# A hybrid mixer in a fused two-block kernel: attention heads taken in pairs, mask and pattern counts added in PSUM by TensorE, and the attention half of the output product multiplied first

## The chip, the cores and the metric

The kernel runs on one core of one Trainium2 chip. The metric is the device time of one execution in microseconds (us); smaller is better. Before the change the median of three runs was 2360.88 us, the lowest 2359.72 and the highest 2361.94.

## What is computed

One program holds two networks' blocks on 256 tokens of width 1024: a first block (retention, a gated spatial unit, and two expert layers that gather rows from memory) and then a second block. The change is in the hybrid mixer of the second block only:

```
def hybrid_mixer(h, w_in, conv_w, g_attn_out, g_conv_out, w_out):
    proj = h @ w_in                                   # 1024 -> 6 x 512
    q, k, v, bg, cg, xc = jnp.split(proj, 6, axis=-1) # 8 heads of 64
    for window, dilation in ((128, 1), (512, 4), (2048, 16)):
        o, lse = dilated_window_attention(q, k, v, window, dilation)
    attn = sum over patterns of softmax(lse) * o
    conv = bg * causal_conv3(cg * xc, conv_w)
    merged = concatenate([rms_norm(attn, g_attn_out), rms_norm(conv, g_conv_out)])
    return merged @ w_out
```

Mixing the three patterns by their softmax denominators is the same as one softmax in which a key that lies in n of the patterns counts n times (n is 1, 2 or 3), and a key in none counts zero. The kernel uses that form: one score row of 256 keys for each query and head, `exp(s) * many` in the numerator and in the sum. Since the sequence is 256 long and causal, the first 128 queries see 128 keys and the last 128 see 256: 384 columns for each head.

## The kernel before

Each of the five engines runs its own instruction list, in the order in which the code issues it; an instruction waits for semaphores and whatever stands behind it on that engine waits too. There is no scheduler: the order is that of the code.

**Weights.** Every weight matrix is cut into blocks of 512 rows by 512 columns (1 MB in float32). SyncE loads them in one fixed order into a ring of four slots, `ring`, and waits for the block four places back to be used. For a product of nearly float32 accuracy each block is split in two: ScalarE rounds it to a high part (`highs`, L1840), VectorE subtracts it from the block to get the low part (`lows`, L1102), and TensorE multiplies high by high, high by low and low by high. `block_after(mat, n)` is the last block of chunk n of a matrix plus two, so a call `highs(block_after(...))` splits up to two blocks ahead of the chunk that is multiplied. I number the blocks of the hybrid stage from its first: chunks 2, 0, 1, 4, 5, 3 of `w_in` (in that order) are blocks 0 and 1, 2 and 3, 4 and 5, 6 and 7, 8 and 9, 10 and 11; `w_out` is 12 to 15, and `q_mem` of the next stage begins with 16 and 17. A chunk of `w_in` is two blocks of 48 matmuls each (`columns_product`, L659); one block of `w_out` is 24 matmuls of 512 columns (`tile_product`, L611).

**PSUM.** Three double banks, `pair0` to `pair2`, are handed out in the order of `sums_in_order`; a sum may open only when the third one before it has been read (`open_sum`, `taken_sum`). Two single banks `small0` and `small1` are handed out in the order of `small_in_order` in the same way.

**The hybrid stage.** Chunk 2 gives v, 0 gives q, 1 gives k, 4 gives the gate cg, 5 the value xc and 3 the gate bg. Attention takes one head at a time: TensorE makes scores (`att_scores`, L943); VectorE adds the mask, finds the row maximum (`att_max`, L1622 to L1628); ScalarE takes the exponential (`exponentials`, L2099); VectorE multiplies by the pattern counts and sums (`att_sum`, L1635); TensorE transposes three tiles (`att_turn`, L931), ScalarE copies them to SBUF (`take_turned`, L1912), TensorE multiplies with v (`att_out`, L957 to L959), and VectorE scales the 64 columns into `b_att` (`att_step`, L1648). Heads 0 to 2 start between the chunks, heads 3 to 7 follow after the last chunk. GpSimd computes the convolution from `b_uT` (`convolution`, L523 to L535) once VectorE has made it (L1669) and, for its last two operations, once chunk 3 is there. After head 4 TensorE sums its squares over the partitions (`conv_sq`, L985), VectorE and ScalarE normalise it and split it (L1678 to L1691, L2120, L1847), so the convolution half of the merged rows is the first to be multiplied by `w_out` (`k_order` reverses that matrix). The attention half follows when its rows are normalised (L1697 to L1707), transposed (`att_rows`, L996) and split. Then `product_by_halves` (L1229, L1233) adds each 512 columns to x and makes the rows `b_h` that the memory stage transposes (L691).

## Time and profile before

| What | Value |
|---|---|
| Median of three runs | 2360.88 us |
| Lowest and highest | 2359.72 and 2361.94 us |
| The profiled execution, its own time | 2357.6 us |
| Its span, from the first to the last instruction | 2355.7 us |
| Mean granted TensorE clock | 0.964 of full |
| TensorE busy | 2000.7 us, 85% |
| VectorE busy | 1579.6 us, 67% |
| ScalarE busy | 1015.7 us, 43% |
| GpSimd busy | 607.4 us, 26% |

The span is 1.9 us shorter than the time of the same execution, and that execution lies 3.3 us below the median of the three timed runs. The hybrid stage is a small part: its q, k and v are ready at 2000.6 us and its second output chunk is summed at 2102.75 us. Shares over the whole span say nothing about so short a stage; it has to be read by windows and instruction by instruction.

### The profile page before, as it was taken

To read this page: it belongs to the slowest core of one execution; us is meant where nothing else is said; L and a number is where in the kernel's file an instruction comes from. 1 tells how busy PE (TensorE), PEld (TensorE's weight loads), DVE (VectorE), ACT (ScalarE), POOL (GpSimd) and SP (SyncE) were. 2 spreads that over 40 slices of the span, in tenths; PEclk is the share of its full clock that TensorE was granted. 3 is DMA by queue.
4 is the path that set the end of the run, shared out by engine and by line. 5 is a ranking of instruction groups with operands and counts; after the bars stand their busy time and mean duration, and the time that the engine had idled before them with its cause. 6 is when DMAs were issued, how large, how long until landed. Compare 5 with 4: busy or idle time off the path is not lost. (4 is left out here: it accounts for less than half of the span.)

```text
span 2355.7 us, 23854 instructions
## 1 busy us (share of the span) xinstructions
PE 2000.7 (85%) x8004; PEld 1247.9 (53%) x8004; DVE 1579.6 (67%) x2973; ACT 1015.7 (43%) x2119; POOL 607.4 (26%) x562
## 2 busy tenths in 40 slices
PE   3998879878777778799977988888887878989998
PEld 2976665322222223379866543433432326868987
DVE  7875766676667766578776676666677654565654
ACT  3342344444444444334334554444454444344543
POOL 0000024443434444200002444444444340400000
PEclk9999899999999999999988999999999999889999
DMA  7775579999999999786566999999999994333553
GB/s 296 283 295 205 214 290 421 421 421 421 421 421 420 422 421 418 304 315 239 190 225 236 421 421 421 420 421 421 421 408 422 421 421 155 117 116 119 186 181 141
DMA packets 112634, 761.93 MB, mean 323 GB/s; under 512 B 12880, under 2 KB 13664, under 8 KB 26368
## 3 DMA queue, kind: packets, MB, share of 16 engines
q0 software_dynamic: 76720, 549.67, 56.3%
q1 hardware_dynamic: 34832, 207.73, 23.7%
q10 hardware_dynamic: 960, 3.01, 0.4%
q8 instruction: 63, 1.03, 0.2%
q14 instruction: 59, 0.48, 0.1%
HBM read 759.32 MB, written 1.05 MB: 323 GB/s over the span
## 5 line engine op out<-in xcount | busy, mean ns | idle before, releaser
L855 PE MATMUL pair<-uv,p_diag 128*128 128x512 f32 x1536 | 758.7, 629 | 200.1 <-ACT p_diag L2024 199.2
L1436 DVE CUSTOM_DVE_ANT_0 uv<-uv,p_h 128x1024 f32<-128x1024 f32 x384 | 470.5, 1225 | 339.9 <-DMA uv<-in_peer_uv,p_idx 339.4
L513 POOL DMA_INDIRECT uv<-in_peer_uv,p_idx x384 | 430.2, 1120 | 764.5 <-PE pair L855 592.8
L855 PEld LDWEIGHTS pair<-uv,p_diag 128*128 128x128 f32 x1536 | 278.2, 195 | 658.0 <-ACT p_diag L2024 398.2
L1102 DVE TENSOR_TENSOR ring_low<-ring,ring_high 128x2048 fp32r<-128x2048 f32 x148 | 336.5, 2288 | 149.2 <-ACT ring_high L1840 144.7
L2018 ACT ACTIVATE p_act<-p_dot 128x1 f32<-128x1 f32 x512 | 103.6, 202 | 664.6 <-DVE p_dot L1436 662.4
L1840 ACT ACTIVATE ring_high<-ring 128x2048 fp32r<-128x2048 f32 x148 | 278.8, 1908 | 195.9 <-DMA ring<-in_ret_w_in 47.3
L659 PE MATMUL pair<-hT_high,ring_high 128*128 128x256 f32 x1056 | 306.9, 291 | 2.6 <-DVE hT_low L1112 2.5
L659 PE MATMUL pair<-hT_low,ring_high 128*128 128x256 f32 x1056 | 301.1, 285 | 0.0
L659 PE MATMUL pair<-hT_high,ring_low 128*128 128x256 f32 x1056 | 300.9, 285 | 0.0
L855 PE MATMUL pair<-uv_high,p_diag 128*128 128x512 f32 x512 | 249.0, 618 | 39.1 <-ACT p_diag L2024 39.1
L2024 ACT ACTIVATE p_diag<-ident,p_w 128x128 f32<-128x128 f32 x512 | 205.6, 402 | 16.9
L1436 DVE CUSTOM_DVE_ANT_0 uv_high<-uv_high,p_h 128x1024 f32<-128x1024 f32 x128 | 156.7, 1224 | 80.4 <-DMA uv_high<-in_peer_uv,p_idx 79.3
L659 PEld LDWEIGHTS pair<-hT_high,ring_high 128*128 128x128 f32 x1056 | 205.0, 194 | 6.9 <-issue 5.7
L659 PEld LDWEIGHTS pair<-hT_low,ring_high 128*128 128x128 f32 x1056 | 205.1, 194 | 2.5 <-issue 2.4
L659 PEld LDWEIGHTS pair<-hT_high,ring_low 128*128 128x128 f32 x1056 | 204.7, 194 | 0.0
L855 PEld LDWEIGHTS pair<-uv_high,p_diag 128*128 128x128 f32 x512 | 93.1, 194 | 190.0 <-ACT p_diag L2024 105.0
L2020 ACT ACTIVATE p_w<-p_act,p_gate 128x1 f32<-128x1 f32 x512 | 150.7, 294 | 51.1 <-ACT p_act L2018 3.0
L513 POOL DMA_INDIRECT uv_high<-in_peer_uv,p_idx x128 | 136.4, 1066 | 129.3 <-PE pair L855 116.8
L611 PE MATMUL pair<-ring_high,hT_high 128*128 128x512 f32 x240 | 98.7, 411 | 6.7 <-DVE ring_low L1102 5.2
L611 PE MATMUL pair<-ring_high,hT_low 128*128 128x512 f32 x240 | 95.5, 398 | 0.0
L611 PE MATMUL pair<-ring_low,hT_high 128*128 128x512 f32 x240 | 95.4, 397 | 0.0
(343 smaller groups left out, 2267.7 us busy)
## 6 DMA issues: line engine op xcount, KB each, us to landing
ada<-in_ada_w SPq DMA_DIRECT2D x50, 512.0 KB, 5.8
ring<-in_ret_w_in SPq DMA_DIRECT2D x24, 1024.0 KB, 5.7
ring<-in_sgu_w_in SPq DMA_DIRECT2D x24, 1024.0 KB, 6.9
ring<-in_peer_w_query SPq DMA_DIRECT2D x16, 1024.0 KB, 4.8
ring<-in_w_up SPq DMA_DIRECT2D x16, 1024.0 KB, 4.8
ring<-in_w_down SPq DMA_DIRECT2D x16, 1024.0 KB, 4.8
mod<-in_ada_w SPq DMA_DIRECT2D x30, 512.0 KB, 6.1
ring<-in_sgu_w_out SPq DMA_DIRECT2D x12, 1024.0 KB, 5.3
```

The lines of the kernel that those rows point to most:

```text
L513: nc.gpsimd.indirect_dma_start(uv_rows[SLOT[l][s]].rearrange("p a d -> p (a d)"), None, experts, bass.IndirectOffsetOnAxis(ap=p_idx[:, k:k ...
L611: mm = nc.tensor.matmul(acc[:, t, :], a, b[:, k, :], start=(first and k == 0 and j == 0), stop=(last and k == BK - 1 and j == 2))
L659: mm = nc.tensor.matmul(acc[:, nt // 2, nt % 2 * S:(nt % 2 + 1) * S], a[:, k, n_tile], b[:, kk, :], start=(kk == 0 and nt % 2 == 0 and j = ...
L855: mm = nc.tensor.matmul(acc[:, half, :], p_diag[:, n % DIAGS, :], v[:, half * 512:(half + 1) * 512], start=(k == 0), stop=(k == PICKS - 1))
L1102: did(V.tensor_tensor(ring_low[:, i % R], ring[:, i % R], ring_high[:, high_at[i]].bitcast(F32), ALU.subtract), w_low, i + 1)
L1436: V.tensor_tensor_reduce(out=u, in0=u, in1=p_h[:, s // PICKS, :], scale=1.0, scalar=0.0, op0=ALU.mult, op1=ALU.add, accum_out=p_dot[:, n % ...
L1840: did(A.activation(ring_high[:, high_at[i]], ring[:, i % R], ACT.Copy), w_high, i + 1)
L2018: did(A.activation(p_act[:, d:d + 1], p_dot[:, d:d + 1], ACT.Gelu_apprx_tanh))
L2020: did(A.activation(p_w[:, d:d + 1], p_act[:, d:d + 1], ACT.Copy, scale=p_gate[:, s % PICKS:s % PICKS + 1]))
L2024: did(A.activation(p_diag[:, n % DIAGS, :], ident[:], ACT.Copy, scale=p_w[:, d:d + 1]), diag_ready, n + 1)
```

## The change

Heads are taken in pairs (`ATT_PAIRS = 4`). For a pair both heads' scores stand in one double bank, one head in each bank. A matmul of the identity with `b_mask` first writes the mask into PSUM and the scores are added to it. The mask table now holds 8 ln(n) where a key lies in n patterns (8 is the inverse of the score scale) and -1e30 elsewhere, so the exponential comes out already multiplied by n; `b_many`, its load, the mask addition and the count multiplication on VectorE are gone. VectorE reads the maxima of both heads straight from PSUM in two reductions, ScalarE takes four exponentials straight from PSUM, each with its own row sum, and the double bank is given back only when `att_sum` has seen them. Chunks 4, 5 and 3 are each multiplied in two halves with attention work between the halves. The blocks of `w_out` are interleaved (chunk 0 and chunk 1 of the attention rows, then both of the convolution rows), the attention half is multiplied first for both chunks, and the normalisation of the convolution moves behind it.

```diff
-    out += [("w_in", 2), ("w_in", 0), ("w_in", 1), ("att", 0), ("w_in", 4), ("att", 1), ("w_in", 5), ("att", 2), ("w_in", 3)]
-    out += [("att", h) for h in range(3, HEADS)]
+    out += [("w_in", 2), ("w_in", 0), ("w_in", 1), ("att", 0), ("att", 1), ("w_in", 4), ("att", 2), ("w_in", 5), ("att", 3), ("w_in", 3)]
...
-                        pool.dma_start(b_many, w["att_many"]).then_inc(hyb_in, 16)
...
+                def att_scores(b):
+                    name = ("att", b)
                     open_sum(name)
...
+                    for j in range(2):
+                        lo = j * HD
+                        half = sum_of(name)[:, j, :]
+                        for t in range(TT):
+                            keys = (t + 1) * P
+                            to = half[:, t * S:t * S + keys]
+                            nc.tensor.matmul(to, ident[:], b_mask[:, t * P:t * P + keys], start=True, stop=False, skip_group_check=True)
+                            mm = nc.tensor.matmul(to, b_qT[lo:lo + HD, b, t * P:(t + 1) * P], b_kT[lo:lo + HD, b, 0:keys],
+                                                  start=False, stop=True, skip_group_check=True)
                     mm.then_inc(sum_ready, 1)
...
                 att_scores(0)
-                columns_product(("w_in", 4), ("w_in",), 4, hT)
+                chunk(4, 0)
                 att_scores(1)
+                chunk(4, 1)
                 att_turn(0)
-                columns_product(("w_in", 5), ("w_in",), 5, hT)
+                att_scores(2)
+                chunk(5, 0)
                 pe.wait_ge(*taken_sum(("w_in", 2)))
...
+                att_out(0)
+                att_turn(1)
+                chunk(5, 1)
+                att_scores(3)
+                att_turn(2)
+                chunk(3, 0)
+                att_out(1)
+                att_out(2)
+                att_turn(3)
+                chunk(3, 1)
+                att_out(3)
...
+                for c in range(2):
+                    open_sum(("w_out", c))
+                    for t in range(TT):
+                        mm = out_tile(c, 0, t)
+                    mm.then_inc(w_used, 1)
+                    if c == 0:
                         pe.wait_ge(sq_ready, 1)
                         open_small(("conv_sq",))
...
+                pe.wait_ge(mcv_ready, 2)
+                for c in range(2):
                     for t in range(TT):
...
+                        if c == 1 and t == 1:
+                            for tile in range(TT):
+                                turn_group(7, b_h, tile, 0)
+                        mm = out_tile(c, 1, t)
+                    mm.then_inc(sum_ready, 1)
...
+                def att_sum(b):
+
+                    stat = b_stat[:, b % 2]
+                    dve.wait_ge(e_ready, 4 * (b + 1))
+                    dve.sem_inc(taken_sum(("att", b))[0], 1)
+                    did(V.reciprocal(stat[:, 3, :], stat[:, 2, :]))
...
                 att_max(0)
+                lows(block_after(("w_in",), 4) - 1)
+                att_max(1)
+                lows(block_after(("w_in",), 4))
                 att_sum(0)
-                lows(block_after(("w_in",), 4))
-                att_max(1)
+                att_max(2)
+                lows(block_after(("w_in",), 5) - 1)
+                att_sum(1)
+                att_take(0)
                 lows(block_after(("w_in",), 5))
...
+                lows(out_first + 5)
                 product_by_halves(7, ("w_out", 0), 0, x_gain)
-                lows(block_after(("w_out",), 1))
                 lows_hT(7, ((0, 0), (1, 0)))
...
+                exponentials(0)
+                highs(block_after(("w_in",), 4) - 1)
+                exponentials(1)
+                highs(block_after(("w_in",), 4))
+                take_sum(("w_in", 4), columns(b_cgT))
+                take_turned(0)
+                exponentials(2)
+                highs(block_after(("w_in",), 5) - 1)
+                take_turned(1)
...
-    mask = np.where(many > 0, 0.0, NEG).astype(f)
+    mask = np.where(many > 0, np.log(np.maximum(many, 1)) * HD ** 0.5, NEG).astype(f)
```

What stands on ScalarE in a row, from the copy of k out of PSUM onward. `b_sm` are the masked scores of a head before; `b_e` are the exponentials of a pair after, `b_stat` its maxima and sums; `ring_high` is the high part of a weight block, `b_cgT` the gate cg. Before:

```order
L1916 ACTIVATE b_kT<-pair 128x1024
L2099 ACT_TABLE_LOAD
L2099 ACTIVATE b_sm<-b_sm,head_even 128x128
L2099 ACTIVATE b_sm<-b_sm,head_even 128x256
L1840 ACTIVATE ring_high<-ring 128x2048 x2
L1916 ACTIVATE b_cgT<-pair 128x1024
```

And in the changed kernel:

```order
L1939 ACTIVATE b_kT<-pair 128x1024
L2124 ACT_TABLE_LOAD
L2124 ACTIVATE b_e,b_stat<-pair,b_stat 128x128 x2
L2124 ACTIVATE b_e,b_stat<-pair,b_stat 128x256 x2
L1863 ACTIVATE ring_high<-ring 128x2048
L2124 ACTIVATE b_e,b_stat<-pair,b_stat 128x128 x2
L2124 ACTIVATE b_e,b_stat<-pair,b_stat 128x256 x2
L1863 ACTIVATE ring_high<-ring 128x2048
L1939 ACTIVATE b_cgT<-pair 128x1024
L1935 ACTIVATE b_pT_even<-small 128x384 x2
L2124 ACTIVATE b_e,b_stat<-pair,b_stat 128x128 x2
L2124 ACTIVATE b_e,b_stat<-pair,b_stat 128x256 x2
```

The two high parts (blocks 8 and 9) that stood together are now apart, each behind the four exponentials of a pair; the next one, of block 10, stands behind those of pair 2.

What stands on VectorE in the same stretch, with the buffers' numbers (`ring_low` is the low part of a block). Before:

```order
L1639 RECIPROCAL head_even<-head_even 128x2
L1102 TENSOR_TENSOR ring_low_49<-ring,ring_high 128x2048 x2
L1622 TENSOR_TENSOR b_sm_145<-pair1,b_mask_149 128x128
L1622 TENSOR_TENSOR b_sm_145<-pair1,b_mask_149 128x256
L1626 TENSOR_REDUCE head_odd<-b_sm_145 128x1 x2
L1628 TENSOR_SCALAR head_odd<-head_odd 128x2
```

And in the changed kernel, from the maxima of pair 1 on:

```order
L1648 TENSOR_REDUCE b_stat_150<-pair0 128x2 x2
L1651 TENSOR_SCALAR b_stat_150<-b_stat_150 128x4
L1128 TENSOR_TENSOR ring_low_49<-ring,ring_high 128x2048
L1658 RECIPROCAL b_stat_150<-b_stat_150 128x4
L1648 TENSOR_REDUCE b_stat_150<-pair2 128x2 x2
L1651 TENSOR_SCALAR b_stat_150<-b_stat_150 128x4
L1128 TENSOR_TENSOR ring_low_49<-ring,ring_high 128x2048
L1658 RECIPROCAL b_stat_150<-b_stat_150 128x4
L1665 TENSOR_TENSOR b_att_148<-small0,b_stat_150 128x2x128
L1128 TENSOR_TENSOR ring_low_49<-ring,ring_high 128x2048
L1690 TENSOR_TENSOR b_uT_140<-pair0,b_cgT_139 128x4x256
```

The reciprocals are those of `att_sum`, which also gives the bank of its pair back. Pair 1's scores lie in `pair0`, and so does chunk 5 (the last row reads it from there); between them stand the maxima of pair 2 and the low part of block 10.

What stands on VectorE at the end of the stage, from the squares of the convolution on. Before, from the low part of the attention rows:

```order
L1112 TENSOR_TENSOR b_m_low<-small,b_m_high 128x4x128 x2
L1102 TENSOR_TENSOR ring_low<-ring,ring_high 128x2048 x2
L1229 TENSOR_TENSOR x<-x,pair 128x512
L1233 TENSOR_TENSOR b_h<-x,gain 128x512
L1229 TENSOR_TENSOR x<-x,pair 128x512
L1233 TENSOR_TENSOR b_h<-x,gain 128x512
L1102 TENSOR_TENSOR ring_low<-ring,ring_high 128x2048 x2
```

And in the changed kernel:

```order
L1138 TENSOR_TENSOR b_m_low<-small,b_m_high 128x4x128 x2
L1128 TENSOR_TENSOR ring_low<-ring,ring_high 128x2048
L1723 TENSOR_SCALAR b_rs<-small 128x256
L1727 RECIPROCAL b_rs<-b_rs 128x256
L1730 SCALAR_TENSOR_TENSOR b_sq<-b_cv,col,b_rs 128x256 x4
L1138 TENSOR_TENSOR b_m_low<-b_sq,b_m_high 128x1024
L1128 TENSOR_TENSOR ring_low<-ring,ring_high 128x2048 x3
L1255 TENSOR_TENSOR x<-x,pair 128x512
L1259 TENSOR_TENSOR b_h<-x,gain 128x512
```

The normalisation of the convolution has moved in behind the attention rows, and the low parts of blocks 16 and 17, which stood behind the first `product_by_halves`, now stand ahead of it.

## Rows read from the trace of the kernel before

**Rows 1.** Windows: stretch; us; PE, PEld, DVE, ACT, POOL busy; granted clock; DMA share, GB/s.

```profile
2000.50:2026.00 25.50, 25.27 (x203) 24.51 (x204) 13.33 (x24) 11.75 (x12) 0.00 (x0) 1.00 0.46 165
2040.00:2060.00 20.00, 15.44 (x57) 11.03 (x56) 13.38 (x39) 6.96 (x14) 14.91 (x10) 0.60 0.15 54
2060.00:2084.00 24.00, 14.93 (x61) 11.71 (x60) 12.58 (x34) 7.36 (x13) 0.00 (x0) 0.69 0.01 5
```

**Rows 2.** Chain that ended last, in order of time: start, us, what.

```profile
2001.62 11.71 PE pair L659 x96
...
2039.62 0.17 PE small L957 x2
...
2040.23 0.86 PE pair L943 x4
...
2056.79 3.58 PE small L985 x8
...
2075.39 6.96 PE pair L611 x24
...
2084.84 11.43 PE pair L611 x48
```

**Rows 3.** Timeline of PE: start, us, instruction, idle before it and its releaser.

```profile
2013.25 0.92 PE L943 MATMUL pair<-b_kT,b_qT 64*128 64x128 f32 x4
2014.10 0.55 PE L931 MATMUL small<-ident,b_p 128*128 128x128 f32 x3
...
2068.09 0.90 PE L931 MATMUL small<-ident,b_p 128*128 128x128 f32 x3 [5.88 <-DVE head_even L1635]
...
2082.18 1.04 PE L996 MATMUL small<-ident,b_att 128*128 128x128 f32 x8
```

**Rows 4.** Timeline of DVE, 2018 to 2080 us.

```profile
2018.45 4.49 DVE L1102 TENSOR_TENSOR ring_low<-ring,ring_high 128x2048 fp32r<-128x2048 f32 x2 [2.68 <-ACT ring_high L1840]
...
2028.46 0.61 DVE L1626 TENSOR_REDUCE head_even<-b_sm 128x1 f32<-128x128 f32 x2
...
2065.98 1.23 DVE L1112 TENSOR_TENSOR b_m_low<-b_sq,b_m_high 128x1024 fp32r<-128x1024 f32 x1 [1.18 <-ACT b_m_high L1847]
...
2075.82 0.69 DVE L1697 CUSTOM_DVE_ANT_0 b_sq<-b_att 128x512 f32<-128x512 f32 x1
...
2077.86 1.41 DVE L1707 SCALAR_TENSOR_TENSOR b_att<-b_att,rstd,b_ga 128x512 f32<-128x512 f32 x2
```

**Rows 5.** Timeline of DVE and ACT in the memory stage, which reads PSUM directly.

```profile
2118.56 0.69 DVE L1733 TENSOR_REDUCE head_even<-pair 128x2 f32<-128x512 f32 x1 [2.91 <-PE pair L1016]
...
2119.48 0.56 ACT L2141 ACTIVATE n_p<-pair,head_even,rstd 128x256 f32<-128x256 f32 x1 [1.77 <-DVE head_even L1735]
```

**Rows 6.** Timeline of ACT: high parts at the end of the stage.

```profile
2095.61 1.91 ACT L1840 ACTIVATE ring_high<-ring 128x2048 fp32r<-128x2048 f32 x1 [6.29 <-DMA ring<-in_w_q_mem]
```

**Rows 7.** Windows of 2 us, columns as in rows 1.

```profile
2064.00:2066.00 2.00, 0.00 (x0) 0.00 (x0) 0.82 (x4) 1.06 (x1) 0.00 (x0) 0.62 0.00 0
2076.00:2078.00 2.00, 2.00 (x6) 1.52 (x6) 1.60 (x7) 0.20 (x1) 0.00 (x0) 0.50 0.00 0
2078.00:2080.00 2.00, 2.00 (x10) 1.65 (x9) 1.27 (x2) 0.00 (x0) 0.00 (x0) 0.97 0.00 0
```

**Rows 8.** Timeline of POOL, one row of DVE, and the first POOL line (min/median/max ns).

```profile
2048.31 2.35 POOL L530 TENSOR_TENSOR b_cv<-b_cv,b_sq 128x1024 f32<-128x1024 f32 x1
2050.73 2.63 POOL L533 TENSOR_TENSOR b_cv<-b_cv,b_bgT 128x1024 f32<-128x1024 f32 x1
2053.44 1.89 POOL L535 TENSOR_TENSOR b_sq<-b_cv 128x1024 f32<-128x1024 f32 x1
...
2048.80 2.00 DVE L1635 CUSTOM_DVE_ANT_0 b_p<-b_sm,b_many 128x128 f32<-128x128 f32 x1 [0.87 <-ACT b_sm L2099]
...
L523 POOL TENSOR_SCALAR b_cv<-b_uT,col x4: 916/926/4762, 2030.6 to 2037.1; 128x256 f32<-128x256 f32 x4
```

**Rows 9.** Instructions on the tile b_many on POOL (min/median/max ns).

```profile
L505 POOL DMA_DIRECT2D b_many<-in_att_many x1: 597/597/597, 1478.6 to 1478.6; - x1
```

More of the change, by code:

```diff
@@ L51 @@
 LEAD = 7
-CONV_AT = 4
+ATT_PAIRS = 4
 WS_UNIT = 5
@@ L90, in k_order @@
 def k_order(mat, kt):
-    order = list(range(kt // BK))
-    return order[::-1] if mat == ("w_out",) else order
+    return list(range(kt // BK))
 def pick_slots():
@@ L604, in tile_product @@
             def tile_product(acc, mat, n, step, kb, lhs, t, first, last):
-                high, low = split(first_block_of[mat + (n,)] + step)
+                high, low = split(block_of(mat, n, step))
                 for k in range(BK):
@@ L963, in hybrid, with chunk @@
+                def chunk(c, kb):
+                    columns_product(("w_in", c), ("w_in",), c, hT, parts=(kb,))
                 columns_product(("w_in", 0), ("w_in",), 0, hT)
                 columns_product(("w_in", 1), ("w_in",), 1, hT)
+                pe.wait_ge(hyb_in, 16 * 2)
                 for c in range(2):
@@ L1655, in hybrid @@
+                out_first = first_block_of[("w_out", 0)]
                 for c in (2, 0, 1):
@@ L1672, in hybrid @@
                 dve.sem_inc(conv_in_ready, 1)
-                lows(block_after(("w_in",), 3))
-                for h in range(1, CONV_AT + 1):
-                    att_step(h)
+                att_sum(2)
+                att_max(3)
+                lows(out_first)
+                att_take(1)
+                att_take(2)
+                att_sum(3)
+                lows(out_first + 1)
+                att_take(3)
+                for t in range(TT):
+                    did(V.tensor_tensor_reduce(out=b_rows[:, t, :], in0=b_att[:, t, :], in1=b_att[:, t, :],
+                                               scale=1.0, scalar=0.0, op0=ALU.mult, op1=ALU.add, accum_out=hs[:, t:t + 1]))
+                settle()
+                did(V.tensor_scalar(ms[:], hs[:, 0:2], 1.0 / 512, EPS, ALU.mult, ALU.add))
+                settle()
+                dve.sem_inc(cms_ready, 1)
+                dve.wait_ge(croot_ready, 1)
+                did(V.reciprocal(rstd[:], root[:]))
+                settle()
+                for t in range(TT):
+                    did(V.scalar_tensor_tensor(out=b_att[:, t, :], in0=b_att[:, t, :], scalar=rstd[:, t:t + 1], in1=b_ga,
+                                               op0=ALU.mult, op1=ALU.mult), arow_ready, t + 1)
+                for t in range(TT):
+                    name = ("att_rows", t)
+                    low_of(b_mT[1][:, 0:4, t * P:(t + 1) * P], b_mT[0][:, 0:4, t * P:(t + 1) * P],
+                           small_of(name)[:, :].rearrange("p (k t) -> p k t", t=P), name)
+                lows(out_first + 2)
                 name = ("conv_sq",)
@@ L2105, in hybrid @@
-                chunks = ((2, b_v), (0, columns(b_qT)), (1, columns(b_kT)), (4, columns(b_cgT)), (5, None), (3, columns(b_bgT)))
-                for step, (c, dst) in enumerate(chunks):
-                    highs(block_after(("w_in",), c))
-                    if dst is not None:
-                        take_sum(("w_in", c), dst)
-                    if step >= 3:
-                        take_turned(step - 3)
-                    if step >= 2:
-                        exponentials(step - 2)
@@ new lines, in take_turned @@
+                def take_turned(b):
+                    for j in range(2):
+                        name = ("attT", 2 * b + j)
+                        take_small(name, b_pT[b % 2][:, j, :], small_of(name)[:, 0:384])
+                out_first = first_block_of[("w_out", 0)]
+                for c, dst in ((2, b_v), (0, columns(b_qT)), (1, columns(b_kT))):
+                    highs(block_after(("w_in",), c))
+                    take_sum(("w_in", c), dst)
+                exponentials(0)
+                highs(block_after(("w_in",), 4) - 1)
@@ new lines, in hybrid @@
+                exponentials(1)
[5 more added lines that the diff above has]
+                take_turned(1)
+                highs(block_after(("w_in",), 5))
+                take_turned(2)
+                exponentials(3)
+                highs(out_first + 1)
+                take_turned(3)
+                take_sum(("w_in", 3), columns(b_bgT))
```

212 lines of the change are left out of this document (79 added, 133 removed).

## The prediction, made before the change was run

> **What bounds the kernel now.** The change lives in the hybrid stage, so I read that stage and not the shares of the whole span. First the windows. From 2000.5 to 2026 us TensorE is busy for 25.27 of 25.50 us at full clock; from 2040 to 2084, where heads 3 to 7 run with no chunk of weights beside them, it is busy for 30.4 of 44 us, and at a granted clock of 0.60 and 0.69, so much of that busy time is twice as long as at the upper level, 2.4 GHz [rows 1]. Then the chain: while there are chunks it is TensorE throughout; after them it goes around between TensorE, VectorE and ScalarE once a head, and through the normalisation of the convolution, during which TensorE sits for 5.88 us [rows 2, 3]. Those are what the change can win: at most 13.6 us of idleness, and what half clock costs.
>
> The yardstick is one event: TensorE ends the second `w_out` chunk at 2102.75 us: from 2084.84 come 11.43 us of products, the transposes, and the last 24 matmuls [rows 2]. What follows (memory stage, MLP) is untouched and follows TensorE, so a shift there arrives at the end unchanged.
>
> **Prices.** At full clock: a half chunk is half of some 11.6 us, 5.8 [rows 2]. The scores of one head, 384 columns, take 0.85 from the start of the first to the start of the transposes, three transposes 0.48 [rows 3], the product with v 0.61 [rows 2]. A mask matmul is not in this trace. Nearest is `conv_sq`, 128 rows of contraction and float32 like it: 4 x 256 columns in 3.58 us at half clock, so 384 columns at full clock take 0.67 [rows 2]. Below that it can't be: those columns are streamed as any others; above, 0.85, the price of the scores with their start. A pair costs 2 x 0.85 + 2 x 0.67 = 3.0 us (up to 3.4); before, 1.7. Four pairs add 5.4 us of TensorE, 5.2 to 6.8.
> The maxima of a pair read 256 and 512 columns of PSUM: about 0.4 (two reductions of 128 and 256 columns take 0.61 [rows 4]) and 0.69 [rows 5], with the scaling 1.3. Four exponentials with their own sums, at 0.56 each for 256 columns [rows 5]: 2.2, the 128-column ones taken as equal for the reads of the sums that come with each. A high part is 1.9 [rows 6], a low part 2.25 [rows 4].
>
> **Removed.** VectorE loses, for each head, the mask addition and the count product. That shortens a head's round trip where it is bare. The five heads that ran with nothing beside them are now in pairs between half chunks, so the idleness there goes. The convolution's normalisation no longer stops TensorE for 5.88 us between heads.
>
> **Added: a wait inside the chunks.** I follow the new order from 2000.7, when the first scores start as now. Scores 0 to 2003.7, half of chunk 4 to 2009.5, scores 1 to 2012.5, the other half to 2018.3 (its blocks were split earlier), transposes to 2019.2. Scores 2 need pair 0's bank. VectorE gives it back in `att_sum(0)`, behind the maxima of pair 1 and the low part of block 9, whose high part stands behind pair 1's exponentials: 2012.5 + 1.3 + 2.2 + 1.9 + 2.25 = 2020.1. TensorE waits 1 us, and ends scores 2 at 2023.2.
> Now the large one. Chunk 5 is summed in the bank that held pair 1. It is given back in `att_sum(1)`, which stands behind the maxima of pair 2 and the low part of block 10; and the high part of block 10 stands behind pair 2's exponentials. Pair 2's scores have only just ended, so nothing overlaps: 1.3 + 2.2 + 1.9 + 2.25 and some 0.15 of signals, **7.8 us** in which TensorE has nothing, from 2023.2 to 2031.0. Queued behind it are all of chunk 5, the first product with v, and through `b_uT` GpSimd's whole convolution.
>
> **What that wait does to the clock.** After TensorE stops at 2062.2 the granted clock is at 0.62 over 2064 to 2066; the 24 matmuls that start at 2075.39 run at half clock (1.2 GHz) to about 2078 [rows 7] and take 6.96 us, where 48 take 11.43 in the next row [rows 2]: 1.2 us lost, and they had other TensorE work just ahead of them. Straight from idleness it is more: half clock for one more microsecond would be 1.7, for two 2.2. I take 1.7 for a product that starts from idleness and 1.4 for one with transposes ahead. The Trainium skill (TensorE: Matmul & The Clock Gate, section HAM oscillation) describes the same loss, and by its worked case, 1.67 us throttled and half of it lost at each wait, re-entry would cost an estimated 0.83; the sum would be about 1.4 us smaller. The row is from this kernel, so I go by it.
>
> **The rest, step by step.** Half of chunk 5 to 2038.5 (5.8 + 1.7); the product of pair 0 (1.2), six transposes, the last three behind `att_take(0)` (1.5 together), 2040.7 after rounding; the other half 2046.5; scores 3 2049.5; transposes 2050.5; half of chunk 3 2056.3; products of pairs 1 and 2 2058.8; transposes 2059.8; half of chunk 3 2065.6; product of pair 3 2066.8. `att_take` (0.5), then the norm as now: squares start at 2075.82 and the first row is there 0.75 after 2077.86 [rows 4], 2.8 us. Transposes at 2070.1; from their start to the first product it is now 2.66 us [rows 2, 3], plus 0.7 for the later second row and half clock: 2073.5. TensorE has then been nearly idle for 6 us, so 5.6 + 1.4 for the first product: 2080.5. `conv_sq` 1.8, next product 5.6: 2087.9.
> The convolution chain, from the end of `conv_sq` [rows 2] to that of its low part [rows 4], takes from 2060.4 to 2067.2 now, 6.8 us, and ends at 2089.2 with a signal, so TensorE waits 1.3 us. Third product 2094.8, half of the fourth 2097.6. Here it wants `b_h`. But VectorE now splits blocks 16 and 17 first, and block 17 can only be loaded once the second product has freed its slot (2087.9): the load and its signal take about 5.1 (the high part at 2095.61 waited for the same load, freed at 2090.5 [rows 6]), high 1.9, low 2.25, then x and `b_h` of two tiles 3.0: 2100.2, transposes 0.5, and the last half product 2.8: **2103.5**. That is 0.75 us after the present 2102.75.
>
> **GpSimd against VectorE.** VectorE's count product of 128 columns took 2.00 us, from 2048.80 to 2050.80, while GpSimd ran a two-input operation to 2050.66; the other way around, a GpSimd operation whose median is 0.93 us took 4.76 beside two low parts [rows 8]. The convolution now starts at 2048 instead of 2030.6. Its first addition (2.35) falls near 2055.5, where the low part of block 12 wants to start at 2055.6; `att_take(1)` and the transposes of pair 3 queue behind that low part: 1.5 us. Its product with bg (2.63) can only start when ScalarE has copied chunk 3, which is when the last head is taken: the squares, with 0.69 us each, meet it: 2.1 us. Its square (1.89) then meets the row products: 1.2 us. Each costs nothing if VectorE is first. Before, such hits lay in the same stage and are in the measured 2102.75. All three: 4.8 us.
>
> **Load.** `b_many` was one issue of 0.60 us on GpSimd in the gather stream [rows 9]; leaving it out gives 0 to 0.6 us, I take 0.5.
>
> **Sum.** 0.75 + 4.8 - 0.5 = +5.05 us. The profiled execution would take 2357.6 + 5.0 = 2362.6. The median lies 3.3 us above it, so I add to the median: 2360.9 + 5.1 = **2366.0**.
>
> **Rivals.** What this kernel can be told apart by is 0.2%, 4.7 us: faster below 2356.2, slower above 2365.6.
> *The forecast*, three hits as placed, 2364 to 2368.5: chance 0.45, two thirds of it above 2365.6.
> *No hit, no change in time* (0.25): GpSimd's operations fall a microsecond to either side, so that VectorE is first at all three. Against it: the copy of chunk 3 ties the second hit to the last head. For it: both orders are in rows 8. Then 0.75 - 0.5, 2361, with one small hit 2363. It decides when the low part of block 12 starts more than 0.4 us earlier and the squares before the copy ends. The Trainium skill (SBUF — State Buffer, section Who interferes with whom) says that whichever starts first has the port pair for its whole instruction; by that rule the order alone decides, and either result can stand.
> *The clock holds* (0.12): the waits of 7.8 and about 6 us don't lower it. That takes 1.7 + 1.4 + 0.5 = 3.6 back: 2357.5 without hits, and below 2356.2 if the maxima and exponentials of a pair are also a microsecond shorter where TensorE waits for them twice. Against it: TensorE stopped at 2062.2 and the clock was down within 4 us [rows 3, 7].
> *More waiting* (0.18): exponentials at 0.75 each with the reading of their sums add 0.8 at both waits, scores at 3.4 add 4 x 0.4, half clock for 2 us more adds 1: 4.2 us, 2370 with the hits.
>
> **Numbers.** Slower: 0.30 + 0.18 = 0.48. Within: 0.15 + 0.25 + 0.05 = 0.45. Faster: 0.07. The range reaches from one hit less than none, 2359, to the worst case, 2371.
>
> **What would show it.** In the trace after: TensorE idle for 7 to 8 us before the first matmul of chunk 5, with a low part as releaser; granted clock near 0.5 behind it; the low part of block 12, the squares or the row products lasting some 2 us longer than their 2.25, 0.69 and 0.75 and ending with a GpSimd operation; 24 matmuls of the first `w_out` product in 7 us. The step most likely to be wrong is the hits. If TensorE's wait before chunk 5 is under 3 us, I have misread who frees the bank, and the time falls to 2360 or less.

## The result and the profile after

The changed kernel took 2366.49 us, the median of 9 runs (2364.18 to 2369.31); the kernel before took 2359.72 beside it (9 runs, 2354.53 to 2363.92). The ratio is 1.0036, its 95% interval 1.0024 to 1.0047: 5.7 to 11 us slower. The prediction was 2366.0, with slower as the likeliest sign. The total fits; inside it terms were wrong in both directions.

| | before | after |
|---|---|---|
| Span of the profiled execution | 2355.7 us | 2367.5 us |
| Mean granted TensorE clock | 0.964 | 0.962 |
| TensorE busy | 2000.7 us | 2011.9 us |
| VectorE busy | 1579.6 us | 1568.1 us |
| ScalarE busy | 1015.7 us | 1013.6 us |
| GpSimd busy | 607.4 us | 602.6 us |
| Stage: first score to the end of the last w_out matmul | 102.0 us | 111.1 us |
| From there to the end of the program | 253.0 us | 253.0 us |

The last two rows are the instrument for all that follows; "stage" means the first of them, "the rest" the second. The first score matmul stood between 1999 and 2006 us in the profiles, whatever the kernel, so a span from one profile carries several us that the edit did not cause. What lies behind the stage was 253.0 to 253.1 us in all profiles but one (which is told below). So I compare stages, and use the timed ratios as the control.

TensorE's waits from 2003 to 2115 us, in the changed kernel (total, times, longest):

```profile
PE small L1007 <- DVE b_att L1714: 6.7, 1, 6.7
PE pair L662 <- DVEq L1657: 5.0, 1, 5.0
PE pair L614 <- DVE b_m_low L1138: 1.5, 1, 1.5
PE pair L614 <- DVEq L1736: 1.4, 1, 1.4
PE pair L950 <- ACT b_kT L1939: 1.3, 1, 1.3
PE small L694 <- DVE b_h L1259: 1.1, 2, 0.7
PE small L934 <- DVE b_att L1665: 1.1, 2, 0.8
```

The second row is the predicted wait ahead of chunk 5: 5.0 us where 7.8 stood. L1657 is the bare `sem_inc` in `att_sum`, and `DVEq` is VectorE's sequencer, which passes it on. Why it is shorter stands on VectorE's timeline:

```profile
2031.29 1.02 DVE L1648 TENSOR_REDUCE b_stat<-pair 128x2 f32<-128x256 f32 x2 [3.39 <-PE pair L951]
2032.35 0.17 DVE L1651 TENSOR_SCALAR b_stat<-b_stat 128x4 f32<-128x4 f32 x1
2036.10 2.29 DVE L1128 TENSOR_TENSOR ring_low<-ring,ring_high 128x2048 fp32r<-128x2048 f32 x1 [3.58 <-ACT ring_high L1863]
2038.31 0.17 DVE L1658 RECIPROCAL b_stat<-b_stat 128x4 f32<-128x4 f32 x1
```

and TensorE's first matmul of chunk 5:

```profile
2036.19 0.58 PE L662 MATMUL pair<-hT_high,ring_high 128*128 128x256 f32 x1 [5.03 <-DVEq L1657]
```

It starts 0.09 us after the low part of block 10 has *begun*, not after it has ended at 2038.39: the increment, which stands behind that low part in the program, had been passed on by then.

The scores of pair 1, on TensorE's timeline:

```profile
2016.42 0.39 PE L950 MATMUL pair<-b_mask,ident 128*128 128x128 f32 x2
2016.74 0.48 PE L951 MATMUL pair<-b_kT,b_qT 64*128 64x128 f32 x2
2017.15 0.70 PE L950 MATMUL pair<-b_mask,ident 128*128 128x256 f32 x2
2017.78 0.70 PE L951 MATMUL pair<-b_kT,b_qT 64*128 64x256 f32 x2
...
2020.49 0.39 PE L662 MATMUL pair<-hT_high,ring_high 128*128 128x256 f32 x1
```

From the first of them to the chunk (the last row) it takes 4.07 us; the prediction had 3.0, and 3.4 as its upper bound. And pair 0 met something that the prediction had nowhere, the clock. Windows of the changed kernel, columns as in [rows 1]:

```profile
2004.00:2006.00 2.00, 2.00 (x9) 1.09 (x8) 0.00 (x0) 0.47 (x1) 0.00 (x0) 1.00 1.00 422
2006.00:2008.00 2.00, 2.00 (x5) 1.19 (x6) 0.00 (x0) 0.00 (x0) 0.00 (x0) 0.56 0.09 37
2008.00:2010.00 2.00, 2.00 (x8) 1.38 (x7) 1.07 (x3) 0.00 (x0) 0.00 (x0) 0.50 0.00 0
```

TensorE is busy without a gap (it had waited 1.32 us just ahead of pair 0), and its granted clock falls to 0.50, the 1.2 GHz level. Pair 0 and the half chunk behind it took 5.20 + 7.80 = 13.0 us, where 4.07 + 5.86 = 9.9 is what pair 1 and its half chunk took: 3.1 us.

The end of the stage went as placed: squares hit by GpSimd (a "hit" is a VectorE instruction that lasts longer beside one of GpSimd), the first w_out product slow after idleness. Three of GpSimd's operations:

```profile
2061.15 2.39 POOL L533 TENSOR_TENSOR b_cv<-b_cv,b_sq 128x1024 f32<-128x1024 f32 x1
...
2074.22 2.34 POOL L536 TENSOR_TENSOR b_cv<-b_cv,b_bgT 128x1024 f32<-128x1024 f32 x1 [0.71 <-ACT b_bgT L1939]
2076.64 2.22 POOL L538 TENSOR_TENSOR b_sq<-b_cv 128x1024 f32<-128x1024 f32 x1
```

and VectorE beside them:

```profile
2061.15 4.54 DVE L1128 TENSOR_TENSOR ring_low<-ring,ring_high 128x2048 fp32r<-128x2048 f32 x1 [3.59 <-ACT ring_high L1863]
...
2074.90 2.20 DVE L1704 CUSTOM_DVE_ANT_0 b_rows<-b_att 128x512 f32<-128x512 f32 x1
...
2077.04 2.37 DVE L1704 CUSTOM_DVE_ANT_0 b_rows<-b_att 128x512 f32<-128x512 f32 x1
```

The low part of block 12 took 4.54 us instead of 2.29, the two squares 4.57 together instead of 1.38 [rows 4]. What the first of these cost on TensorE stands ahead of the transposes of pair 3:

```profile
2066.17 1.09 PE L934 MATMUL small<-ident,b_e 128*128 128x128 f32 x6 [0.78 <-DVE b_att L1665]
```

The other wait in that row of the table of waits (0.28 us) is at pair 1, before GpSimd had begun.

### The profile page after: what moved, and what is told of

Read it like the earlier page. It is cut to its first block and busy times, and to the rows that moved or that the text cites. A ratio compares the mean times of both kernels' runs of the same rounds, so it can differ in the third digit from the quotient of the medians.

```text
span 2367.5 us, 23840 instructions
## 1 busy us (share of the span) xinstructions
PE 2011.9 (85%) x8036; PEld 1257.3 (53%) x8036; DVE 1568.1 (66%) x2905; ACT 1013.6 (43%) x2133; POOL 602.6 (25%) x561
## 5 line engine op out<-in xcount | busy, mean ns | idle before, releaser
L516 POOL DMA_INDIRECT uv<-in_peer_uv,p_idx x384 | 424.9, 1107 | 768.4 <-PE pair L858 599.6
```

The lines of the kernel that those rows point to most:

```text
L516: nc.gpsimd.indirect_dma_start(uv_rows[SLOT[l][s]].rearrange("p a d -> p (a d)"), None, experts, bass.IndirectOffsetOnAxis(ap=p_idx[:, k:k ...
```

## The experiments

Each is an edit of the changed kernel. "Stage" is the stage of its profile. Experiments 5 to 12 also contain the edit of the first, so they are read against 103.8 us.

**1. The bank given back early.** Does the wait ahead of chunk 5 come from the place of `att_sum(1)`?

```diff
                 att_sum(0)
+                att_sum(1)
                 att_max(2)
                 lows(block_after(("w_in",), 5) - 1)
-                att_sum(1)
```

> The changed kernel with one move on VectorE: att_sum(1), which gives back the bank of pair 1, stands ahead of the maxima of pair 2 and the low part of block 10. I measure the stage from the first score matmul to the end of the second w_out chunk: 102.0 us before, 111.1 us after. Theory (the wait ahead of chunk 5 is on the path): its 5.0 us of idleness go, and the half clock that follows it, 1.9 us; the stage takes 104 to 105 us and the time is 6 to 7 us below the changed kernel, level with before. Rival (slack further down takes it up, since GpSimd's convolution and the last head set the end): the idleness goes but the stage stays above 109 us. Second rival (the bank is not what TensorE waits for): the wait stays at 4 to 5 us and moves to another releaser.

Measured: 2358.52 us, ratio to before 0.9998 (0.9988 to 1.0009), stage 103.8. The wait ahead of chunk 5 is gone (5.0 us), and what its half chunk lost at half clock with it (7.69 to 5.85 us); the first w_out product took 6.99 us instead of 7.40. Together the stage is 7.3 us shorter. This one moved call is the difference between slower and no change. The squares were hit as before.

**2. The squares on ScalarE.** Is the hit by GpSimd worth its 3.2 us?

```diff
-                for t in range(TT):
-                    did(V.tensor_tensor_reduce(out=b_rows[:, t, :], in0=b_att[:, t, :], in1=b_att[:, t, :],
...
+                act.wait_ge(att_done, 1)
+                for t in range(TT):
+                    square(b_att[:, t, :], hs[:, t:t + 1])
...
```

> The changed kernel with the two row sums of squares of the attention rows on ScalarE in place of VectorE, which has to signal and wait for them. Theory (VectorE was held by GpSimd's two-input operations: 2.20 and 2.37 us where 0.69 is its free price): on ScalarE two squares with their sums take some 1.6 us with signals instead of 4.5, and the stage shortens by 2.5 to 3 us, to 108 to 109 us. Rival (the hit only moves): the row products or the reciprocal behind them now meet the last GpSimd operation and lose 1 to 2 us, and the gain is 1 us or less. Second rival (the two squares were slow for a reason of their own): they take 2 us each on ScalarE too.

Measured: 2366.87, ratio 1.0039 (1.0025 to 1.0053), stage 109.9: 1.2 us won, not 2.5 to 3. Each square took 0.63, so they escaped; but ScalarE's timeline shows what stood behind them:

```profile
2071.85 1.28 ACT L2155 ACT_TABLE_LOAD   x1
2073.14 0.20 ACT L2155 ACTIVATE root<-ms 128x2 f32<-128x2 f32 x1
```

The table of the square root, loaded under cover before, now lay on the path. The wait ahead of the row transposes was 1.8 us shorter, but the first w_out product 0.7 us longer (8.12). The timed runs show no gain over the changed kernel (1.0036 for that one).

**3. No mask matmuls** (mask and pattern counts are left out).

```diff
-                            nc.tensor.matmul(to, ident[:], b_mask[:, t * P:t * P + keys], start=True, stop=False, skip_group_check=True)
...
-                                                  start=False, stop=True, skip_group_check=True)
+                                                  start=True, stop=True, skip_group_check=True)
```

> The changed kernel without the 16 mask matmuls: the scores carry neither mask nor pattern counts. It prices the mask. Theory (all four pairs' scores are on the path and a mask matmul costs what a score matmul costs): scores of a pair fall from 4.1 to about 2.1 us, 8 us for four pairs, and if the long stretch of narrow float32 matmuls is what let the clock fall in pair 0, another 3 us go: the stage takes 100 to 103 us and the time falls by 8 to 11 us. Rival (the mask is hidden, since TensorE waits behind pairs 2 and 3 anyway): the gain is 4 us or less. My prediction had 0.67 us for the mask of a head, 5.4 us in all.

Measured: 2355.45, ratio 0.9992 (0.9983 to 1.0002), stage 99.6, 11.5 less than the changed kernel. The clock stayed at 1.00 in pair 0. All scores of pair 0, on TensorE's timeline:

```profile
1999.72 0.93 PE L950 MATMUL pair<-b_kT,b_qT 64*128 64x128 f32 x8 [1.32 <-ACT b_kT L1938]
2000.58 0.39 PE L662 MATMUL pair<-hT_high,ring_high 128*128 128x256 f32 x1
```

Eight records in 0.86 us, where one head's four took 0.85 [rows 3]. Two heads cost what one did: the even head contracts over partitions 0 to 63 and the odd head over 64 to 127, and the two halves of the array worked side by side: one after the other they would take twice the 0.85, by that row. The Trainium skill (TensorEngine Tiling (Array Packing), section Key Properties) says that different tiles can load weights and multiply in parallel; the row agrees. So a mask matmul of 128 partitions between scores costs more than its own columns: a pair took 3.2 us less without, where the four masks by `conv_sq` are 1.34. Four times 3.2 and the 3.1 of the clock are 15.9 us, of which the stage shows 11.5. Later waits took part of it back: the one ahead of the row transposes grew from 6.65 to 9.16 us, and the first w_out product behind it from 7.40 to 8.35.

**4. The bank given back late.** VectorE drains ahead of the increment:

```diff
                     dve.wait_ge(e_ready, 4 * (b + 1))
+                    settle()
                     dve.sem_inc(taken_sum(("att", b))[0], 1)
```

> The changed kernel in which att_sum waits for all VectorE work before it, the low part too, ahead of giving the bank back. My prediction took the bank to be given back when the low part of block 10 has ended, and had 7.8 us of idleness ahead of chunk 5; measured are 5.0, and the low part begins when chunk 5 does. Theory (the increment is passed on when the low part is issued, not when it has ended): with the wait the idleness ahead of chunk 5 becomes 7.2 to 7.4 us, scores of pair 2 wait some 0.8 us, and the stage grows by about 3 us. Rival (the bank was already given back after the low part, and scores ended later than the rows say): nothing changes.

Measured: 2371.0, ratio 1.0053 (1.0038 to 1.0069), stage 114.1. The first matmul of chunk 5:

```profile
2038.64 0.58 PE L662 MATMUL pair<-hT_high,ring_high 128*128 128x256 f32 x1 [7.42 <-DVEq L1658]
```

7.42 us, and 0.85 ahead of scores 2: the two waits of the prediction (7.8 and 1.0) are what this kernel has, and the changed kernel doesn't, because its increment goes out early. One thing more differs. GpSimd's addition and the low part of block 12 begin at the same time, as in the changed kernel, but this time it is the addition that lasts longer.

```profile
2063.33 2.29 DVE L1128 TENSOR_TENSOR ring_low<-ring,ring_high 128x2048 fp32r<-128x2048 f32 x1 [3.59 <-ACT ring_high L1864]
2063.33 4.50 POOL L533 TENSOR_TENSOR b_cv<-b_cv,b_sq 128x1024 f32<-128x1024 f32 x1
```

From the products of pairs 1 and 2 to the next half chunk it took 3.70 us, against 4.41 in the changed kernel: the hit had cost 0.7.

**5. Mask matmuls in one pass.** ScalarE rounds identity and mask to fp32r tiles (so the mask and counts are added at that precision).

```diff
-                            nc.tensor.matmul(to, ident[:], b_mask[:, t * P:t * P + keys], start=True, stop=False, skip_group_check=True)
+                            nc.tensor.matmul(to, b_idr, b_maskr[:, t * P:t * P + keys], start=True, stop=False, skip_group_check=True)
...
```

> The changed kernel with the bank given back early (as in the first experiment), and the mask matmuls in one pass: ScalarE copies identity and mask table into fp32r tiles during chunk 2 and the mask matmuls read those, so the added mask and pattern counts are rounded to fp32r. Stage length of the kernel with only the bank moved: 103.8 us; total 2358.5. Taking the mask matmuls out of the changed kernel made the stage 11.5 us shorter, of which 3.1 were the clock that no longer fell in the midst of pair 0. A one-pass mask should cost a pair some 0.8 us instead of 2.1, so 5.2 us less over four pairs. If the clock falls in pair 0 because of the float32 mask matmuls (theory), it holds here and the stage is 95.5 us, total 2350. If it is any alternation of weights on narrow products, it falls again: 98.6 us, total 2353. If a mask matmul costs by its weight load and not by its passes, nothing moves: 103 us, 2358.

Measured: 2357.21, ratio 0.9989 (0.9975 to 1.0003), stage 100.2. A pair took 3.12 us instead of 4.08, not 2.8. The clock fell all the same in pair 0, so float32 masks are not its cause. This was the expected branch "it falls again", with 1.6 us less won.

**6. Squares on ScalarE, table ahead.**

```diff
                 take_sum(("w_in", 3), columns(b_bgT))
+                root_table()
+                act.wait_ge(att_done, 1)
+                for t in range(TT):
+                    square(b_att[:, t, :], hs[:, t:t + 1])
...
```

> The bank given back early, and the squares of the attention rows on ScalarE with the square root's table loaded ahead of them (a dummy square root behind the copy of chunk 3). Theory: the squares lose 3.2 us to GpSimd's last two operations, and the squares on ScalarE won only 1.2 before because the table load (1.28 us) fell on the path. Then the stage is 101.0 us against 103.8 with the bank alone, total 2356. Rival: what is won is waited for at the convolution's squares, whose GpSimd operations are no sooner: the first w_out product starts earlier, conv_sq does not, and the stage is 103 us.

Measured: 2361.17, ratio 1.0013 (1.0001 to 1.0026). The stage is 100.9, but in this execution the clock did not fall in pair 0 (4.15 and 5.85 us); with the 3 us that it cost in the others this is 104, nothing won. Two rows say why. VectorE:

```profile
2064.41 1.39 DVE L1706 TENSOR_SCALAR ms<-head_even 128x2 f32<-128x2 f32 x1 [2.40 <-ACTq L2154]
```

GpSimd:

```profile
2063.89 1.89 POOL L539 TENSOR_TENSOR b_sq<-b_cv 128x1024 f32<-128x1024 f32 x1
```

An instruction on two numbers a partition, 0.17 us in other places, took 1.39 and ended with GpSimd's at 2065.8: the hit moved on to the next VectorE instruction. The Trainium skill (SBUF — State Buffer, section Who interferes with whom) counts `tensor_scalar` among those that can take the shared ports; this row agrees. And the first w_out product took 8.26 us, against 6.99 in experiment 1. The wait ahead of the rows was 5.59 against 6.65: a us less idle, and 1.3 us more at half clock.

**7. Low parts of blocks 16 and 17 later.**

```diff
-                lows(out_first + 5)
                 product_by_halves(7, ("w_out", 0), 0, x_gain)
+                lows(out_first + 5)
```

> The bank given back early, and the low parts of blocks 16 and 17 behind the first product_by_halves, as in the kernel before, not ahead of it. Theory: the two waits at the end of the stage (0.33 and 0.74 us) go, the stage is 102.7 us against 103.8, and the first product of q_mem does not start later relative to it: total 2357.5. Rival: the low parts are wanted by q_mem at once, so what is won at the transposes is waited for there: stage 102.7, total 2358.5.

Measured: 2367.89, ratio 1.0035 (1.0021 to 1.0048), stage 109.5. A miss, by an error in the edit: the call also splits block 15, which the fourth w_out product needs. TensorE's timeline:

```profile
2100.78 0.80 PE L614 MATMUL pair<-ring_high,b_m_high 128*128 128x512 f32 x1 [5.11 <-DVE ring_low L1128]
```

**8. All of these together,** with `conv_sq` ahead of the first w_out product.

```diff
+                pe.wait_ge(sq_ready, 1)
+                open_small(("conv_sq",))
...
                 for c in range(2):
                     open_sum(("w_out", c))
...
-                    if c == 0:
-                        pe.wait_ge(sq_ready, 1)
```

> All together: bank given back early, one-pass mask matmuls, squares on ScalarE with the table ahead, low parts of blocks 16 and 17 behind the first product_by_halves, and the sums of the convolution's squares (conv_sq) ahead of the first w_out product, where TensorE waits 1.5 us for the attention rows anyway. Theory: 103.8 - 5.2 - 3.1 - 2.8 - 1.1 - 2.5 = 89.1 us of stage, total 2345. Rival: the savings overlap, since after the last head the attention's norm and GpSimd's convolution both run from the end of chunk 3 (GpSimd needs some 7.5 us from there to its last square): 93 us, total 2349.

Measured: 2356.47, ratio 0.9990 (0.9979 to 1.0001), stage 104.5, against 89 to 93. It carries the error of experiment 7 (5.11 us); `conv_sq` took 3.2 us to the next product at half clock instead of 1.54; and the clock fell in both halves of chunk 4 (7.80 and 7.35). It tells nothing apart.

**9. The norm under chunk 3.**

```diff
                 att_turn(3)
-                chunk(3, 1)
                 att_out(3)
+                chunk(3, 1)
```

with the square root ahead of the copy of chunk 3, and the low part of block 13 behind the row products.

> The bank given back early, and the last pair's product with v ahead of the second half of chunk 3 instead of behind it, so that the attention rows are normalised while TensorE multiplies that half (their square root ahead of the copy of chunk 3 on ScalarE, the low part of block 13 behind the row products on VectorE). Theory: after the last product with v TensorE now waits 7.0 us and then runs the first w_out product partly at half clock (some 7.3 us instead of 5.6). Here the wait is at most 1 us and the clock stays up: 103.8 - 6.0 - 1.7 + 1.2 (the last product with v now waits bare for ScalarE's two copies) = 97.3 us of stage, total 2352. Rival: the convolution becomes the bound, since GpSimd needs the copy of chunk 3 and then 4.6 us, and its chain of 6.8 us after conv_sq is covered by one w_out product only: the wait moves ahead of the convolution's half and the stage is 101 us, total 2355.

Measured: 2356.01, ratio 0.9982 (0.9970 to 0.9995), stage 99.2: 4.6 us won of 6.5. The wait of 6.65 ahead of the row transposes is gone. But the low part of block 13 now stands ahead of those of the rows, so TensorE waits 2.79 instead of 1.46, and starts at half clock. Windows:

```profile
2068.00:2070.00 2.00, 0.00 (x0) 0.00 (x0) 2.00 (x3) 2.00 (x3) 2.00 (x1) 0.95 0.77 303
2070.00:2072.00 2.00, 1.39 (x3) 1.16 (x4) 1.95 (x2) 0.53 (x1) 1.92 (x2) 0.50 0.45 188
```

The first w_out product took 8.41 us. The expected "the clock stays up" was wrong: TensorE was idle from 2067.8 to 2070.6, and what followed began at 0.50.

**10. Masks first, then scores.** All four masks of a pair, then its four scores; each bank is opened once.

```diff
                     for j in range(2):
                         for t in range(TT):
                             keys = (t + 1) * P
+                            nc.tensor.matmul(sum_of(name)[:, j, t * S:t * S + keys], ident[:], b_mask[:, t * P:t * P + keys],
+                                             start=(t == 0), stop=False, skip_group_check=True)
+                    for j in range(2):
...
+                        for t in range(TT):
```

> The bank given back early, and within a pair all four mask matmuls first, then all four score matmuls (the accumulation flag opens each bank once). With the mask matmuls gone the scores of a whole pair took 0.86 us, as much as those of one head before: the even and the odd head's 64-row matmuls ran side by side. With a 128-row mask matmul between them a pair took 4.08 us, 3.22 more. Theory: most of that is not the mask's columns but that no two score matmuls are neighbours any more; four float32 masks in a row cost 1.34 us (from conv_sq, 1024 columns in 1.79), so a pair takes 2.2 us, and the stage is 103.8 - 4 x 1.9 = 96.2 us, up to 98.5 where later waits take some back; total 2351 to 2353. Rival: each mask matmul costs by itself what it cost (0.42 and 0.63 us, 2.1 a pair), so a pair takes 3.0 us and the stage is 99.5 us. The clock in pair 0 is open: it fell there in seven profiles of eight with masks.

Measured: 2350.64, ratio 0.9962 (0.9949 to 0.9974), stage 94.8. Pair 1, on TensorE's timeline:

```profile
2014.60 1.48 PE L947 MATMUL pair<-b_mask,ident 128*128 128x128 f32 x8
2016.01 0.93 PE L955 MATMUL pair<-b_kT,b_qT 64*128 64x128 f32 x8
2016.87 0.39 PE L662 MATMUL pair<-hT_high,ring_high 128*128 128x256 f32 x1
```

2.27 us for the same eight matmuls that took 4.07: masks 1.41, scores 0.86. The order of the instructions (the opening flag is set once a bank with it) is worth 1.8 us a pair, and the clock stayed up behind pair 0 (half chunk in 5.85). The four masks cost nearly what `conv_sq` had said (1.34).

**11. All mended:** experiments 10, 5 and 9, with only blocks 16 and 17 split behind `product_by_halves`.

```diff
-                lows(out_first + 5)
+                lows(out_first + 3)
                 product_by_halves(7, ("w_out", 0), 0, x_gain)
+                lows(out_first + 5)
```

> Masks first and in one pass (fp32r copies of identity and mask), the bank given back early, the norm under the second half of chunk 3, and the low parts of blocks 16 and 17 (but not that of block 15) behind the first product_by_halves. Theory, if these add up: a pair's scores 1.3 us (0.4 + 0.86), so 103.8 - 4 x 2.8 - 6.5 - 1.1 = 85 us of stage, total 2340. Rival: with scores this short the maxima, exponentials and splits of VectorE and ScalarE bound the stretch up to chunk 3, and the convolution bounds the end: 92 us, total 2347.

Measured: 2343.33, ratio 0.9934 (0.9918 to 0.9951), stage 84.2, a pair in 1.41 to 1.50. But the rest is 257.15, the one that is not 253.0. TensorE's waits behind the stage:

```profile
PE pair L663 <- DVE hT_low L1143: 2.3, 1, 2.3
```

**12. The low parts ahead again,** as the change has them.

```diff
-                lows(out_first + 3)
+                lows(out_first + 5)
                 product_by_halves(7, ("w_out", 0), 0, x_gain)
-                lows(out_first + 5)
```

> The kernel before this one, with the low parts of blocks 16 and 17 again ahead of product_by_halves, where the change put them. Theory: behind it they stand between b_h and its own low part (hT_low), so the memory stage's first product waited 2.3 us more and ran 1.8 us of its time at half clock: from the end of the stage to the end of the program it took 257.15 us, against 253.0 in every other kernel. Ahead of it the transposes wait again (0.5 and 0.7 us, so the stage is 85.4 us against 84.2), but the rest is 253.0: 2.9 us less in all, 2340.5. Rival: the stage now ends so early that the memory stage waits for the load of q_mem whatever VectorE's order, and the rest stays at 256 to 257 us: 2344.

Measured: 2342.56, ratio 0.9931 (0.9910 to 0.9951), stage 85.8, rest 253.07. By the profiles 2.5 us better than the one before; the timed runs can't tell the two apart. Both beat the changed kernel by some 23 us and the kernel before by some 16.

## Why the prediction came out right, and where it was not

**The wait ahead of chunk 5** was there, from the bank and place named, with chunk 5 behind it: shown by experiment 1 (gone when the call moves) and experiment 4. Its size was wrong. The step "It is given back in `att_sum(1)`, which stands behind the maxima of pair 2 and the low part of block 10" took the increment to go out when the low part ends; it was out when the low part began, and the terms 7.8 and 1.0 became 5.0 and 0: 3.8 us too much. Experiment 4, where it does go out at the end, has 7.42 and 0.85, so 3.2 of these are the increment and the rest are prices a little too high. The re-entry behind it was 7.7 us for the half chunk, 1.9 lost of a predicted 1.7.

**The scores** were mis-sized: "A pair costs 2 x 0.85 + 2 x 0.67 = 3.0 us (up to 3.4)" was 4.07, 4.3 us more over four pairs. The bound "above, 0.85, the price of the scores with their start" priced each matmul by a row in which its neighbours were of its own kind. Experiment 10 shows that it is the alternation: the same matmuls in another order take 2.27, less than 3.0, since there the scores of both heads cost what one head's did.

**The clock in pair 0,** 3.1 us, was in no term. It fell in the midst of unbroken work in eight of the nine profiles in which mask and score matmuls alternate, and in none of the five others (before, and experiments 3, 10, 11 and 12). Alternation alone is not enough: pairs 1 to 3 alternate too, and the half chunk behind them kept to 5.8 to 5.9 us wherever no wait came between, but for pair 1 of experiment 8 (7.35). Only pair 0 has a wait of 1.32 us just ahead of it; the five others have such a wait too (1.16 in the kernel before). Where mask and score alternate a pair also takes longer (3.1 us or more at full clock, against 2.3 or less), and no run holds these two apart. So what in it the chip reacts to is open, and so is why experiment 6 escaped.

**The hits** of 4.8 us were 0.7 ahead of the transposes of pair 3 (predicted 1.5), 3.2 at the squares (2.1) and 0 at the row products (1.2): 3.9. GpSimd's last operation, its square, met VectorE's second square and not the row products. That VectorE's instructions grew beside GpSimd's is shown, and for the first of them that its absence wins the 0.7 (experiment 4); that taking the squares away wins 3.2 is not, since experiments 2 and 6 won 1.2 and nothing.

**The end of the stage** held: 3.43 us from the row transposes to the first product (3.4), 7.4 for that product (7.0), 30.1 from there to the end of the second chunk (30.0). In the last of these two errors cancel: TensorE waited 1.1 us for `b_h` (0.33 and 0.74), not the 2.6 that the working has between 2097.6 and 2100.2, and its products took longer.

**The sum.** The stage was to grow by 0.75 + 4.8 = 5.55 us and grew by 9.1: + 4.3 (scores) + 3.1 (clock) - 3.8 (waits) + 0.2 (half clock behind the wait) - 0.9 (hits) is 2.9 of the 3.5 between them, and 0.4 more is the norm of the rows beyond its hit. The working also has a slip: 2038.5 + 1.2 + 1.5 is 2041.2, not 2040.7; it did little, since the two took 2.36 us and 2.2 were entered. The medians differ by 6.8 us, with an interval of 5.7 to 11 that holds 9.1 and not 5.05. So the predicted time was nearer than its sum deserved, by luck: the terms that were too small and the one that was too large partly cancel, and the sum was added to 2360.88, where the kernel before measured 2359.72 beside the changed one. The 0.5 us for the load of `b_many` can't be seen under a stage start that moves by several us.

**Where the expected gain went.** The change did what it says: no bare round trips of heads. From the first score to the last product with v it took 70.5 us against 74.0, though some 17 us were given away in it by three causes: 4 x 1.8 by the order of mask and score, 3.1 by the clock, 6.9 by one call that held a bank. Experiment 10 shows none of the three and is some 9 us faster than before (ratio 0.9962); with the masks in one pass and the norm under chunk 3 as well (experiments 11 and 12) it is 16.

## What to carry to other kernels

Price a matmul with its neighbours: here 64-row products on the two halves of the array ran side by side when nothing of 128 rows stood between them (0.86 us for two heads), and a pair with masks between them took 1.8 us more than one with the masks ahead, so group by kind. When a sum is given back by an engine with a long queue, look for what stands ahead of that call, and put the call as soon as its data is ready. To compare edits of a short stage, measure from an event at its start to one at its end, and let the timed runs confirm.

## What the runs showed of the hardware beyond that

- A semaphore increment that stands alone behind a 2.29-us VectorE instruction had released TensorE 0.09 us after that instruction began (5.03 us of wait; 7.42 with a drain ahead of it). No data was at risk here, since the program waits for ScalarE's four exponentials, the last to read the bank, ahead of the increment.
- The first w_out product of 24 matmuls took 6.99 to 8.35 us in the nine profiles in which it follows a wait of 4.8 to 9.2 us ahead of the rows, and not in the order of the waits. Behind 6.65 us it was 6.99 (experiment 1) and 7.40 (the changed kernel), behind 9.16 it was 8.35 (experiment 3), but behind the shorter ones of 5.59 and 4.83 (experiments 6 and 2) it was 8.26 and 8.12. So a us less of pause can be paid for by a us more at half clock.
- GpSimd's four single-input operations took 7.39 us instead of 3.67 where they met the end of one low part and the whole of the next (the latter took its 2.29). Beside GpSimd's two-input addition the low part took 4.54 in the changed kernel, and in experiment 4 it took 2.29 and the addition 4.50.
